# Two transformer blocks with product-key experts on one core: the last tile's expert choice moved into the second block, and twenty row units moved from attention to the channel mixer

## The reference

```python
q = (xb @ w_q).reshape(PEER_BLOCK, PEER_HEADS, 2, PEER_HALF)
s = jnp.einsum('thjd,hjkd->thjk', q, sub_keys)        # 8 heads, 2 key sets of 128 keys
sv, si = lax.top_k(s, PEER_TOPK)                      # 16 best keys of each set
cand = sv[:, :, 0, :, None] + sv[:, :, 1, None, :]
cs, ci = lax.top_k(cand.reshape(PEER_BLOCK, PEER_HEADS, PEER_TOPK * PEER_TOPK), PEER_TOPK)
eidx = i1 * PEER_N_KEYS + i2                          # 16 of 16384 experts a head
g = jax.nn.softmax(cs, axis=-1)
act = jax.nn.gelu(jnp.einsum('td,thkd->thk', xb, u))  # u, v = expert_u[eidx], expert_v[eidx]
return jnp.einsum('thk,thkd->td', (g * act), v)
```

## Time and profile before

| | us |
|---|---|
| median of 3 runs | 3019.01 (3010.56 to 3028.56) |
| the profiled execution | 3031.93 |
| its span in the trace | 3030.2 |
| TensorE busy | 2395.2 (79%) |
| VectorE busy | 1747.8 (58%) |
| ScalarE busy | 575.0 (19%) |
| GpSimd busy | 1214.1 (40%) |
| mean granted TensorE clock | 0.877 of full speed |

### The profile page before, as it was taken

How to read it: one execution, slowest core, us unless ns; L and a number is a source line. 1 busy time by engine, 2 the same in 40 slices (tenths; PEclk the granted TensorE clock), 3 DMA queues, 4 the chain that set the end, 5 groups by cost and what they waited for, 6 DMA issues and landing times. The chain is left out here.

```text
span 3030.2 us, 28174 instructions
## 1 busy us (share of the span) xinstructions
PE 2395.2 (79%) x9768; PEld 1672.6 (55%) x9768; DVE 1747.8 (58%) x3622; ACT 575.0 (19%) x1560; POOL 1214.1 (40%) x1058
## 2 busy tenths in 40 slices
PE   6988899889746866998786953774887836999988
PEld 5847788565644545885552732351764312556755
DVE  3315410279998877476777778768786795000510
ACT  4412300112322220000122102321132000112321
POOL 0000000005887657375554766765665672000000
PEclk9998999989978877999898966887968856999999
DMA  3331233338999999799978897988998996342366
GB/s 144 139 135 42 87 139 142 129 141 340 414 364 351 357 336 406 298 418 414 363 266 297 325 411 292 356 329 352 415 367 331 414 410 259 111 161 101 150 234 245
DMA packets 173229, 832.05 MB, mean 275 GB/s; under 512 B 20881, under 2 KB 21137, under 8 KB 156193
## 3 DMA queue, kind: packets, MB, share of 16 engines
q0 software_dynamic: 147456, 536.94, 46.4%
q1 hardware_dynamic: 25632, 293.33, 24.7%
HBM read 828.09 MB, written 2.10 MB: 274 GB/s over the span
## 5 line engine op out<-in xcount | busy, mean ns | idle before, releaser
L1192 POOL DMA_INDIRECT expert_rows<-in_peer_u,chosen x512 | 666.4, 1302 | 1028.6 <-DVE chosen L1768 668.3
L1192 POOL DMA_INDIRECT expert_rows<-in_peer_v,chosen x512 | 544.2, 1063 | 281.1 <-issue 144.4
L1266 DVE SCALAR_TENSOR_TENSOR expert_rows<-expert_rows,u 128x1024 f32<-128x1024 f32 x512 | 602.3, 1221 | 71.4 <-DMA expert_rows<-in_peer_u,chosen 49.1
L2910 PE MATMUL mlp_up<-mlp_xT,mlp_slab 128*128 128x384 f32 (+1 forms) x1024 | 248.2, 399 | 72.9 <-issue 68.0
L1226 PE MATMUL expert_sum<-expert_rows,expert_diag 128*128 128x512 f32 x496 | 244.3, 640 | 32.1 <-ACT expert_diag L1213 23.5
L1276 DVE SCALAR_TENSOR_TENSOR h<-expert_rows,expert_coef,h 128x1024 f32<-128x1024 f32 x194 | 251.5, 1296 | 9.2 <-DMA expert_rows<-in_peer_v,chosen 4.7
L1276 DVE SCALAR_TENSOR_TENSOR u<-expert_rows,expert_coef,u 128x1024 f32<-128x1024 f32 x190 | 246.3, 1296 | 12.6 <-DMA expert_rows<-in_peer_v,chosen 6.1
L2910 PEld LDWEIGHTS mlp_up<-mlp_xT,mlp_slab 128*128 128x128 f32 x1024 | 162.7, 199 | 163.0 <-issue 100.6
L2901 PE MATMUL mlp_down<-mlp_slab,upT 128*128 128x512 f32 x512 | 230.5, 604 | 26.4 <-issue 26.4
L691 PE MATMUL product<-uT,in_slab 128*128 128x272 f32 (+1 forms) x1024 | 237.7, 388 | 8.2 <-DMA in_slab<-in_w_in 8.2
L691 PEld LDWEIGHTS product<-uT,in_slab 128*128 128x128 f32 x1024 | 191.7, 191 | 39.7 <-issue 8.7
(11 more groups left out here) (545 smaller groups left out, 3281.5 us busy)
## 6 DMA issues: line engine op xcount, KB each, us to landing
in_slab<-in_w_in SPq DMA_DIRECT2D x34, 2048.0 KB, 7.6
mix_slab<-in_w_in SPq DMA_DIRECT2D x16, 2048.0 KB, 9.1
mlp_slab<-in_w_up SPq DMA_DIRECT2D x16, 2048.0 KB, 8.3
mlp_slab<-in_w_down SPq DMA_DIRECT2D x16, 2048.0 KB, 7.8
expert_rows<-in_w_in SPq DMA_DIRECT2D x9, 2048.0 KB, 7.6
mix_slab<-in_ssd_w_out SPq DMA_DIRECT2D x8, 2048.0 KB, 8.2
out_slab<-in_w_out SPq DMA_DIRECT2D x6, 2048.0 KB, 8.3
mix_slab<-in_sc_w_out SPq DMA_DIRECT2D x4, 2048.0 KB, 8.7
```

Source lines behind the costliest of these rows:

```text
L1192: pool.indirect_dma_start(out=self.row(n), out_offset=None, in_=self.tables[0 if dot else 1], in_offset=bass.IndirectOffsetOnAxis(ap=picks ...
L1266: dve.scalar_tensor_tensor(self.row(n), self.row(n), 1.0, u, ALU.mult, ALU.mult, accum_out=dot).then_inc(self.rows_used, 1)
L2910: ins = pe.matmul(bank[n % UPS][:, 0:W], slab[i % R][:, k, j * P:(j + 1) * P], xT[:, k, :], start=k == 0, stop=k == KD - 1)
```

## The change

- `CHOICES` for the second route becomes `NOW`, tile three's two choices. Tile four's choice, made with eight heads at once before, is made in two parts of four heads (`LATER`), by VectorE at the head of the first `merge_two` (tiles one and two), before its first gate; ScalarE takes their two exponentials first in that stage. The best scores and their places of both tiles are kept until then in a buffer `best_held`; the temporary room is in `qaT` and `qbT`, which that stage no longer needs. The code of a choice, unchanged in its instructions, moves into the functions `choosing`, `take_exponents`, `sixteen` and `choose`.
- `SETS_J` 3 to 4: 64 units instead of 48 in the second route's search loop, so 18 instead of 34 beside and after the choices. TensorE's units become 114 instead of 124.
- `PLAN_TWO`: the third tile's attend takes 8 units instead of 24, its merge_two 6 instead of 10. The mixer has 191 left instead of 171. `GELU_AT` 9 to 11.
- The first slab of half 1's project is loaded in half 0's last norm_turn, into a buffer of its own (`in_slab_early`), behind the keys and the first query slabs.
- attend's buffers `probs` and `probsT` are only as wide as the tiles so far.

```diff
-SETS_S, SETS_Q, SETS_F, SETS_J = 5, 8, 16, 3
+SETS_S, SETS_Q, SETS_F, SETS_J = 5, 8, 16, 4
 
 CHOICES = ((0, 0, 4), (0, 4, 8), (1, 0, 8))
 
-BEFORE_EXP = (5, 12, 24)
-
-
-PLAN_TWO = (20, 72, 22, 86, 48, 8, 8, 36, 24, 10, 4, 3)
+NOW, LATER = ((0, 0, 4), (0, 4, 8)), ((1, 0, 4), (1, 4, 8))
+
+BEFORE_EXP = (5, 12)
+
+
+PLAN_TWO = (20, 72, 22, 86, 48, 8, 8, 36, 8, 6, 4, 3)
...
+                early.append((third.enter_context(nc.sbuf_tensor("in_slab_early", [P, KD, SLAB], F32, side="right"))[:],
+                              sem("in_landed_early", keep=True)))
...
+                    held.append(holding.enter_context(nc.sbuf_tensor("best_held", [P, 2, 2 * PH * TOPK], F32, side="right"))[:])
...
-                norm_turn("ffn_", part_h[half], None, xT, 0, row_gain_dram=t["ln_ffn"], keep=u[half], bg=bg, ahead=first)
+                coming = [] if half else [(early[0][0], t["w_in"][in_slab(O_Z)], early[0][1])]
+                norm_turn("ffn_", part_h[half], None, xT, 0, row_gain_dram=t["ln_ffn"], keep=u[half], bg=bg,
+                          ahead=first + coming)
...
+            last_choice = None
+            if now and first == 0:
+
+                widths = (64, 64, 256, 320, 448, 128, PH * TOPK + TOPK // 2, PH)
+                ends = list(accumulate(widths))
+                place = qbT[:].rearrange("p h n -> p (h n)")
+                rooms = [qaT[:].rearrange("p a n -> p (a n)")] + [place[:, e - n:e] for e, n in zip(ends, widths)]
+                last_choice = choosing(rooms, [None, held[0][:, 0, :]], [None, held[0][:, 1, :].bitcast(U32)], small.count,
+                                       chosen1, weight1, sem("last_centred"), sem("last_exped"), chosen_ready, slots=64)
...
-                      [(gain[:], t["post_norm_mix_2"].partition_broadcast(P).rearrange("p a d -> p (a d)"), gain_in)])
+                      [(gain[:], t["post_norm_mix_2"].partition_broadcast(P).rearrange("p a d -> p (a d)"), gain_in)],
+                      last_choice)
...
-        slab = [sbuf(ctx, f"in_slab{i}", [P, KD, SLAB]) for i in range(2)]
+        slab = ([early[0]] if half else []) + [sbuf(ctx, f"in_slab{i}", [P, KD, SLAB])[:] for i in range(1 if half else 2)]
...
-            for s in range(2):
-                sp.dma_start(slab[s][:], parts[0][0](s)).then_inc(landed[s], 16)
-            slab_loader(sp, [s[:] for s in slab], landed, product, 4, parts)
+
+            for s in range(1 if half else 0, 2):
+                sp.dma_start(slab[s], parts[0][0](s)).then_inc(landed[s], 16)
+            slab_loader(sp, slab, landed, product, 4, parts)
...
+def take_exponents(act, n, c, part):
+
+    _, h0, h1 = part
+    act.wait_ge(c.centred, n + 1)
+    act.activation(c.top[:, 0:h1 - h0, :], c.top[:, 0:h1 - h0, :], ACT.Exp).then_inc(c.exped, 1)
...
+def choose(dve, chain, n, c, part_of):
+
+    m, h0, h1 = part_of
+    H, heads, slots, count_ = h1 - h0, slice(h0, h1), slice(h0 * TOPK, h1 * TOPK), (h1 - h0) * TOPK
...
-                for n in range(len(CHOICES)):
+                for n in range(len(parts)):
...
+            for n, part in enumerate(parts):
+                choose(dve, chain, n, c, part)
...
-        p_ = [sbuf(ctx, f"probs{i}", [P, S + 1]) for i in range(4)]
-        pT = [sbuf(ctx, f"probsT{i}", [P, S]) for i in range(2)]
+        p_ = [sbuf(ctx, f"probs{i}", [P, (first + T) * P + 1]) for i in range(4)]
+        pT = [sbuf(ctx, f"probsT{i}", [P, (first + T) * P]) for i in range(2)]
...
+            if choice:
+                chain = Chain(dve, step)
+                chain.mark(dve.tensor_copy(choice.count_b, choice.count[:]))
+                for n, part in enumerate(LATER):
+                    choose(dve, chain, n, choice, part)
...
+            for n, part in enumerate(LATER if choice else ()):
+                take_exponents(act, n, choice, part)
...
-    GELU_AT = 9
+    GELU_AT = 11
```

240 lines of the change are left out of this document (127 added, 113 removed).

## The result

The changed kernel is slower: 3046.03 us, the median of 6 runs (3028.43 to 3058.22), against 3017.71 us for the kernel before (6 runs, 3010.56 to 3030.9). The ratio is 1.0081, 95% interval 1.0053 to 1.0109, so +24 us. I had forecast 2996, faster, and given 0.30 to slower; the range, 2925 to 3047, just holds the median. The profiled execution of the changed kernel has a span of 3056.2 us, 26.0 more than before's 3030.2.

The account below looks back on a forecast made before the run. Expert-row gathers were taken to set the middle's pace, with TensorE slowed for 130 us in the mixer. Mixer's start -2 and its stretch -21 gave -23: 3009 for the profiled execution, 2996 against the median, range 2925 to 3047.

Parts of the forecast that it names:

- part 6: Three-tile mixer: 20 more units, but TensorE's slow stretch starts one instruction block later, 105 us instead of 130: -21.
- part 5: Third tile's attend: eight of the 11 steps that have units lose theirs: -12 (bounds -9 and -18).
- Part 1: Second project: TensorE's 14.13 us wait for its first slab goes, but the stage waits for VectorE: 0.
- Parts 2 and 3: Second route: longer search loop +12.5, tail without the third choice on VectorE -29; together -16.5.
- Part 4: First merge_two: the choice, 31 us in two halves, delays w_out: +26.5 (bounds +20.5 and +35.5).
- Mixer's start: Start of the three-tile mixer, summed from the stages ahead: -16.5 + 26.5 - 12 = -2.
- 0.855: Mixer: us lost for each us of slow stretch, where TensorE starts one instruction every 1.40 us.
- Rival (A): Mixer: stretch starts as now, lasts while gathers fill the DMA engines, 25 us longer: +19, 3038; chance 0.22.
- (D): merge_two's choice at its upper bound, search loop +20, mixer's stretch adding 8.5: 3042; chance 0.08.
- holds up nobody: Mixer: the GELU, moved to ScalarE's step 11 and run at 2404 instead of 2381.99, delays no engine.

Follow-up runs that it names:

- e13: The kernel before, unchanged, run again in a set without slow stretches: 2806.02 us, ratio 0.9982 to the kernel before.
- e14: The changed kernel, unchanged, run again in a set without slow stretches: 2828.36 us, ratio 1.0059 to the kernel before.
- e10: The changed kernel with a GpSimd pause ahead of every second gather of the mixer: ratio 1.0071 to the kernel before.
- e5: The changed kernel with a GpSimd pause ahead of each gather of the mixer: 2900.83 us, ratio 0.9632 to the kernel before.
- e1: The changed kernel with PLAN_TWO and GELU_AT of before; choice move, search loop and early slab stay: 3021.61 us, ratio 1.0006 to the kernel before.
- e18: The changed kernel with PLAN_TWO and GELU_AT of before, in a set without slow stretches: 2821.42 us, ratio 1.0067 to the kernel before.
- e17: The kernel before with the changed PLAN_TWO and GELU_AT alone, in a set without slow stretches: 2811.39 us, ratio 1.0043.
- e8: The kernel before with a GpSimd pause ahead of every second gather of the mixer, in a set with slow stretches: 2883.06 us, ratio 0.9566.
- e15: The kernel before with a GpSimd pause ahead of every second gather of the mixer, in a set without slow stretches: 2810.83 us, ratio 0.9989.
- e7: The kernel before with a GpSimd pause ahead of every gather, block one's too: 2908.48 us, ratio 0.967.

## Why the prediction was wrong

On the profiled pair the forecast was -23 up to the fourth tile and +25.4 came. Of the 48 us between them, 39 are the mixer's term (part 6: -21 forecast, +18.2 measured) and 9 the third tile's attend (part 5).

- **Part 1, early slab, 0.** Right. TensorE's project starts 6.6 us earlier in the changed trace (658.5 for 665.1) and ends 3.2 later (875.2 for 872.0), no more than it had drifted before (+2.6 at the first norm_turn). From the first norm_turn to the second, e13 takes 810.1 us, e14 810.8 and e10 810.0.
- **Parts 2 and 3, route, -16.5.** Right: -16.5 in the first pair (+4.4 to -12.1), -14.3 in e14 against e13. Split where the first choice opens, part 2 is +9.9 (e14: +11.8) for +12.5 and part 3 -26.4 (-26.1) for -29, so the exact hit is in part two errors of 3 us that cancel.
- **Part 4, merge_two, +26.5.** Right: +25.4 to norm_twice's start in the first pair, +27.8 in e14. The choice took 31.3 us for the 31 of the forecast. (Less the 5.2 that lay between the stage's opening and the first gate already, 31 makes 25.8, not the 26.5 of the sum.)
- **Part 5, third attend, -12.** Wrong, -2.7 (-2.6 in e14). The step that failed is "the 16.6 us more fall on the 11 steps that have units". I compared two stages whose granted clocks were 0.56 and 1.00 and put the whole difference down to the units. With them gone, TensorE at its lower level and ScalarE behind it took 3.1 us a head. e5, with the same units at 0.80, took 12 us less; and e1 and e18, which keep the 24 units, took 63.6 and 64.5, no more than the changed kernel, so even the 2.7 are not shown to be the units'.
- **Mixer's start, -2.** It came out at +7.2. The 9.2 us between are part 5; the rest, block one (+4.4), norm_twice to latent_heads (-4.8), the third tile's project (+2.8) and smaller ones, cancels.
- **Part 6, the forecast itself.** The formula held: the mixer's +18.2 is near the 20 that 0.855 gives for 23 us more of slow stretch. The step that failed is the reading that a stretch hangs on TensorE's blocks of instructions and would start one block later, at 2459, and so be 25 us shorter. One did begin at 2455, by luck: a first one of 31 us had come ahead of it, both together are 23 us longer than before's, and in a set with the same program there was none at all. The blocks can be seen, too. In before, narrow windows find q8's packets near 2331, 2384, 2546 and 2592 us, and none from 2386 to 2545. Between the second and the third TensorE ran 255 records of both kinds, between the first two 246, between the last two 247. So each packet follows some 250 records, in the slow stretch as outside it, and none came late. Rival (A), the stretch as long as gathers fill the DMA engines, came nearest in mechanism: 3038 predicted, 3046 measured, and 20 units cost the mixer 17 to 24 us in every pair of traces with stretches. (D)'s 3042 is nearer as a number, by terms that didn't come (the search loop at +20, the choice at its upper bound). (A), too, took the stretches for a property of the kernel. Why TensorE slows down is open.
- **The GELU "holds up nobody".** Wrong in both directions. Beside a slow stretch VectorE idled 20 us for it. In e17, without one, ScalarE waited for the dots instead (16.24 us ahead of the GELU), and TensorE did not notice.
- **What I hadn't priced at all:** TensorE's last part of the mixer waits for the last addition. In e13 TensorE had some 28 us to spare there (34 us later it waited 6.1); 20 units take 34. What they then cost is 8 to 9 us (342.4 to 343.5 for 334.2). In before's first trace the slow stretch hid this limit, since TensorE was 111 us behind.
- **The Trainium skill, "Runtime: NRT & Kernel Launch", "Instruction fetch mechanics"** (blocks of 256 instructions fetched while the engine runs the block before, mostly hidden): nothing measured contradicts it, and the even spacing of q8's packets in before, by records and not by time, bears it out against my reading. e13 fetched 5 packets on q8 for 1325 TensorE records and lost nothing.

Order of sizes, where no stretch disturbs: route -14, merge_two +28, attend -3, mixer +8, which makes +19. Measured was +16 (e14, 8 to 25) and +20 (e10, with pauses), and 25 between the traces of e14 and e13, 4.8 of them from ahead of the change. The choice move was meant to use VectorE's idle 22.62 us in merge_two, but of these only 5.2 lay inside the stage; the other 17.4 were at the end of attend, where the choice doesn't run.

## What to carry to other kernels

An idle gap of an engine at a stage's border belongs to two stages: before moving work into it, split it at the barrier, and count only what lies behind the point where the moved work may start. A stage's time with and without background work may be compared only at the same granted clock. And before a forecast is hung on one strange stretch of one trace, the unchanged kernel has to be run again in another set: the largest term here, 111 us, came and went with the set in which the kernel ran.

## What the runs showed that I had not expected

**A 4.3% gain from waiting.** In a set with slow stretches a pause ahead of every second gather of the mixer took the kernel from 3014.93 to 2883.06 us (e8), and in one without them the same kernel cost nothing (e15: 0.9989, 0.9972 to 1.0005). e8 is the version to keep of these: it beats both kernels where there are slow stretches, and equals the kernel before where there are none. It doesn't bring the two kinds of sets together, though. e8 and e15 are one program, 72 us apart, with the mixer at 334.2 us in both: between their traces some 38 us arise in the second half of block one up to the norm_turn, 14 in route and 26 from there to merge_two. e7 has almost no "issue" waits left (19.9 us of them on TensorE, 91.8 in e8, 11.9 in e13) and is no faster. What the stretches ahead of the mixer cost is not shown.

**Engines in step.** In the changed kernel's first slow stretch not only TensorE limps. The timeline of all engines there:

```profile
2394.28 1.22 DVE L1294 SCALAR_TENSOR_TENSOR expert_rows<-expert_rows,u 128x1024 f32<-128x1024 f32 x1 [1.31 <-issue]
2394.30 0.29 PEld L2972 LDWEIGHTS mlp_up<-mlp_xT,mlp_slab 128*128 128x128 f32 x1 [2.51 <-issue]
...
2395.69 0.08 DVE L1294 DVE_READ_ACCUMULATOR expert_rows<-expert_rows,u 128x1 f32 x1 [0.18 <-issue]
2395.70 0.80 PE L2972 MATMUL mlp_up<-mlp_xT,mlp_slab 128*128 128x384 f32 x1 [2.00 <-issue]
...
2397.09 1.22 DVE L1294 SCALAR_TENSOR_TENSOR expert_rows<-expert_rows,u 128x1024 f32<-128x1024 f32 x1 [1.32 <-issue]
2397.10 0.29 PEld L2972 LDWEIGHTS mlp_up<-mlp_xT,mlp_slab 128*128 128x128 f32 x1 [2.51 <-issue]
```

From 2393 to 2400 us VectorE's starts fall on the same 1.40 us steps as TensorE's, to 0.02 us, with "issue" as the reason for both. Two engines that share no semaphore at that point are let on together, so what they wait for may be shared there. In this stretch it is so only there. From 2372 to 2391 us TensorE limps while VectorE keeps its own step of 1.28 us, and during TensorE's pause of 43.24 us VectorE's additions start every 1.24 us. Many packets alone don't bring it about either: e13 had 113 a us with TensorE at its full pace. The clock is no explanation: the 49 records of such a stretch would take 38 us at the lower level. The Trainium skill, "NOTIFIC — the notification-queue block", section 7.1, says that the internal pipeline of the block which writes the engines' trace records holds its producers back rather than lose one; that would fit two engines in step, less well one that stands still while the other runs. No run here turned the records off, and it stays a guess. So does what differs between the two groups of sets.
